# Five pairs of column groups a layer by seven block products instead of three, in both feed-forward layers of a one-core kernel

## What is computed

```python
def squared_relu_mlp(h, w1, w2):          # h 256 x 2048, w1 2048 x 8192, w2 8192 x 2048
    z = jax.nn.relu(h @ w1)
    return (z * z) @ w2
...
        x = x + squared_relu_mlp(rms_norm(x, ffn_norm[i]), w_ff1[i], w_ff2[i])
```

## Time and profile before

| | us |
|---|---|
| median of 3 runs (2959.05 to 2961.48) | 2959.76 |
| the profiled execution's own time | 2960.76 |
| its span, first to last instruction | 2959.0 |
| TensorE busy | 2916.3 |
| VectorE busy | 2055.5 |
| ScalarE busy | 1616.3 |

### The profile page before, as it was taken

How to read it: one execution, slowest core, us unless ns; L and a number is a source line. 1 busy time by engine, 2 the same in 40 slices (tenths; PEclk the granted TensorE clock), 3 DMA queues, 4 the chain that set the end, 5 groups by cost and what they waited for, 6 DMA issues and landing times.

```text
span 2959.0 us, 35189 instructions
## 1 busy us (share of the span) xinstructions
PE 2916.3 (99%) x12996; PEld 2400.2 (81%) x12996; DVE 2055.5 (69%) x2679; ACT 1616.3 (55%) x2134; POOL 634.5 (21%) x1257
## 2 busy tenths in 40 slices
PE   8999999999999999999999999999999999999998
PEld 7888888888888778788788888888888887878887
DVE  6547777777866777876777777756557777887555
ACT  6435555555554566755555555545444446775433
POOL 0003312213043310013203122133324663100210
PEclk9999999999999999999999999999999999999999
DMA  7546777778777655556777778776876776666774
GB/s 263 165 151 203 237 248 250 246 244 255 243 223 243 205 170 164 164 174 203 228 256 253 251 242 253 246 219 211 239 216 200 219 227 190 207 206 206 249 254 157
DMA packets 358156, 649.53 MB, mean 220 GB/s; under 512 B 38624, under 2 KB 63584, under 8 KB 357216
## 3 DMA queue, kind: packets, MB, share of 16 engines
q1 hardware_dynamic: 312976, 578.89, 61.7%
q0 software_dynamic: 44432, 67.45, 7.2%
q10 hardware_dynamic: 576, 0.94, 0.1%
HBM read 598.89 MB, written 10.49 MB: 206 GB/s over the span
## 4 chain that ended last, share of the span: by engine, by line
PE 73%; DVE 14%; DMA 7%; ACT 4%; issue 2%; DVEq 0%; ACTq 0%
PE acc L2093 21%; PE acc L2095 21%; PE acc L2094 21%; DMA raw<-in_w_ff 6%; DVE wlo L1457 5%; ACT whi L1086 1%; DVE wlo L1450 1%; PE tp L2130 1%; PE tp L2132 1%; PE tp L2131 1%; DVE mkv L1472 1%; DVE ob L1900 1%; PE tp L2299 1%; PE sd L2193 0%; PE sd L2218 0%
## 5 line engine op out<-in xcount | busy, mean ns | idle before, releaser
L1457 DVE TENSOR_TENSOR wlo<-raw,whi 128x1024 fp32r<-128x1024 f32 x920 | 1110.7, 1220 | 548.4 <-ACT whi L1086 544.0
L2093 PE MATMUL acc<-whi,set_hi 128*128 128x512 f32 x3696 | 1459.4, 395 | 20.8 <-DVE wlo L1457 15.4
L2095 PE MATMUL acc<-whi,set_lo 128*128 128x512 f32 x3696 | 1440.3, 390 | 0.0
L2094 PE MATMUL acc<-wlo,set_hi 128*128 128x512 f32 x3696 | 1439.8, 390 | 0.0
L1086 ACT ACTIVATE whi<-raw 128x1024 fp32r<-128x1024 f32 x920 | 959.4, 1057 | 684.1 <-PE acc L2095 378.3
L2093 PEld LDWEIGHTS acc<-whi,set_hi 128*128 128x128 f32 x3696 | 694.8, 188 | 182.8 <-DVE wlo L1457 27.1
L2095 PEld LDWEIGHTS acc<-whi,set_lo 128*128 128x128 f32 x3696 | 694.5, 188 | 146.2
L2094 PEld LDWEIGHTS acc<-wlo,set_hi 128*128 128x128 f32 x3696 | 695.0, 188 | 143.3 <-issue 1.9
L1050 POOL DMA_DIRECT2D u<-u x832 | 406.8, 497 | 1447.5 <-DVE u L1648 1337.9
L1450 DVE SCALAR_TENSOR_TENSOR wlo<-raw,par,whi 128x512 fp32r<-128x512 f32 x160 | 111.7, 747 | 47.1 <-ACT whi L1089 46.3
L1089 ACT ACTIVATE whi<-raw,par 128x512 fp32r<-128x512 f32 x160 | 104.2, 715 | 22.4 <-PE acc L2095 10.9
(11 more groups left out here) (332 smaller groups left out, 2121.3 us busy)
## 6 DMA issues: line engine op xcount, KB each, us to landing
raw<-in_w_ff SPq DMA_DIRECT2D x560, 512.0 KB, 4.7
raw<-in_w_in SPq DMA_DIRECT2D x248, 512.0 KB, 4.5
raw<-in_w_out SPq DMA_DIRECT2D x96, 512.0 KB, 4.4
u<-u POOLq DMA_DIRECT2D x832, 32.0 KB, 4.2
raw<-in_w_mem_kv SPq DMA_DIRECT2D x32, 512.0 KB, 4.3
raw<-in_w_proj_a SPq DMA_DIRECT2D x32, 512.0 KB, 4.7
raw<-in_w_proj_b SPq DMA_DIRECT2D x32, 512.0 KB, 6.9
raw<-in_w_kv SPq DMA_DIRECT2D x48, 256.0 KB, 3.3
```

What stands on the lines that cost most here:

```text
L1457: V.tensor_tensor(wlo[:, c], src, whi[:, c].bitcast(f32), ALU.subtract).then_inc(w_lo, 1)
L2093: T.matmul(o, h[:, tok], whi[:, c], start=first, stop=False)
L2094: T.matmul(o, h[:, tok], wlo[:, c], start=False, stop=False)
L2095: ins = T.matmul(o, l[:, tok], whi[:, c], start=False, stop=last)
```

## The change

`PAIRS = (0, 2, 1, 2)` gives the number of pairs in each chunk of a layer, before it was in effect (0, 1, 1, 1). Chunks 1 and 3 are now made by two pairs each and have no whole slab of the first product; chunk 2 stays at one. Pairs of one layer follow each other without a gap, so odd pairs use the PSUM quarters in another order (`bank`), a pair's p1 waits on `part_n2` of the one before and its p5 on `part_n1`, and `part_p1` waits for `part_relu`. The turn of z stands one slab later behind the square, with 7 slabs from turn to split. The diff, cut to what matters:

```diff
 FF2_PAIR = ((0, 1, 2, 3, 4, 5), (6, 7))
+FF2_LATE = ((0, 1, 2, 3), (4, 5), (6, 7))
+FF2_EVEN = ((0, 1), (2, 3), (4, 5), (6, 7))
+
+
+PAIRS = (0, 2, 1, 2)
 
 
 STAGES = ("p1", "p2", "p5", "p3", "p6", "p7", "p4")
...
+    def seven(layer, chunk, src, col, first, last):
+
+        p = sc.pair_of(layer, chunk, src, col, first, last)
+        pair = sc.pairs[p]
+        sc.at("act", pair.end("p1") + 5, "part_p1", p)
+        sc.at("dve", pair.end("p2") + 3, "part_c11", p)
+        sc.at("act", pair.end("p5") + 3, "part_p5", p)
+        sc.at("dve", pair.end("p6") + 3, "part_q", p)
+        return p
+
+    def drain(p, of, rst, z, kt, turn, split):
+
+        pair = sc.pairs[p]
+        add = pair.end("p7") + 3
+        if of == "n1":
+            add = max(pair.end("p4") + 3, add + 5)
+        sc.at("dve", add, "part_" + of, p)
+        sc.at("act", add + 2, "relu_" + of, p, rst)
+        sc.at("act", add + 2, "part_square", p, of, sc.staged, sc.tails)
+        sc.turned(max(turn, add + 3), split, ("staged", sc.staged), z, kt)
+        sc.staged += 1
+        if of == "n2":
+            sc.at("act", add + 3, "part_p7", p, sc.staged)
+
     def ffn(layer, rst, a, z, next_rst, next_gain):
 
-        for c in range(NCHUNK):
-            halved = c > 0
-            gs = [sc.group(f"w_ff1{layer}", 0, D * c + GW * i, a) for i in range(2 if halved else 0, 4)]
+        waiting = []
+        for c, count in enumerate(PAIRS):
+            gs = [sc.group(f"w_ff1{layer}", 0, D * c + GW * i, a) for i in range(2 * count, 4)]
             if c == 0:
                 sc.fed_late(gs[0])
                 v = S * gs[0]
@@ -386,39 +415,36 @@
                 for n in range(4):
                     sc.at("act", v + (13, 14, 16, 17)[n], "sum_hi", layer, n)
                     sc.at("dve", v + (14, 15, 17, 18)[n], "sum_lo", layer, n)
-            else:
+            elif count == 1:
                 v = S * gs[0]
-                pair = sc.pairs[p]
-                for of, kt, add, square, turn, split in (
-                        ("n2", 0, pair.end("p7") + 3, pair.end("p7") + 6, pair.end("p7") + 6, v + 1),
-                        ("n1", 4, pair.end("p4") + 3, pair.end("p4") + 6, v + 2, v + 9)):
-                    sc.at("dve", add, "part_" + of, p)
-                    sc.at("act", add + 1, "relu_" + of, p, rst)
-                    sc.at("act", square, "part_square", p, of, sc.staged, sc.tails)
-                    sc.turned(turn, split, ("staged", sc.staged), z, kt)
-                    sc.staged += 1
-                    if of == "n2":
-                        sc.at("act", square + 1, "part_p7", p, sc.staged)
+                p, = waiting
+                drain(p, "n2", rst, z, 0, f + 11, v + 1)
+                drain(p, "n1", rst, z, 4, v + 2, v + 9)
             for i, g in enumerate(gs):
-                turn, split = S * (g + 1) + 1, S * (g + 2) + 1
-                if halved:
-                    turn, split = S * (g + 1) + 2, S * (g + 2) + 2
-                sc.at("act", S * (g + 1) + 1, "epi_relu2", g, rst, sc.staged, sc.tails)
-                sc.at("act", turn, "epi_square", g, sc.tails)
-                sc.turned(turn, split, ("staged", sc.staged), z, 4 * i + (8 if halved else 0))
+                e = S * (g + 1)
+                late = 1 if count else 0
+                sc.at("act", e + 1, "epi_relu2", g, rst, sc.staged, sc.tails)
+                sc.at("act", e + 1 + late, "epi_square", g, sc.tails)
+                sc.turned(e + 2 + late, e + 9 + late, ("staged", sc.staged), z, 4 * (2 * count + i))
                 sc.staged += 1
             fs = [sc.group(f"w_ff2{layer}", D * c, GW * i, z) for i in range(4)]
-            sc.weave(fs[0], fs[1], FF2_PAIR)
-            if c < NCHUNK - 1:
-                v = S * fs[0]
-                p = sc.pair_of(layer, c + 1, a, v - (14 if halved else 12), v + 26)
-                pair = sc.pairs[p]
-                sc.at("act", pair.end("p1") + 3, "part_p1", p)
-                sc.at("dve", pair.end("p2") + 3, "part_c11", p)
-                sc.at("act", pair.end("p5") + 3, "part_p5", p)
-                sc.at("dve", pair.end("p6") + 3, "part_q", p)
-            for n, left in ((0, 2), (4, 1), (12, 0)):
+            f = S * fs[0]
+            sc.weave(fs[0], fs[1], FF2_PAIR if count < 2 else FF2_LATE)
+            at_need = ((0, 2), (4, 1), (12, 0)) if count < 2 else ((0, 3), (2, 2), (8, 1), (12, 0))
+            for n, left in at_need:
                 sc.groups[fs[n // S]].need[n % S] = [("tail_lo", sc.tails - left)]
+            more = PAIRS[c + 1] if c < NCHUNK - 1 else 0
+            if more == 1:
+                waiting = [seven(layer, c + 1, a, 0, f - (11, 14, 2)[count if c else 0], f + 26)]
+            elif more == 2:
+                sc.weave(fs[2], fs[3], FF2_EVEN)
+                first, middle = (f - 21, f + 6) if c else (f - 11, f + 9)
+                p = seven(layer, c + 1, a, 0, first, middle - 1)
+                q = seven(layer, c + 1, a, 2 * GW, middle, f + 29)
+                drain(p, "n2", rst, z, 0, f + 11, f + 23)
+                drain(p, "n1", rst, z, 4, f + 24, f + 29)
+                drain(q, "n2", rst, z, 8, f + 31, f + 37)
+                drain(q, "n1", rst, z, 12, f + 38, f + 44)
             for i, g in enumerate(fs):
                 e = sc.end(g)
                 sc.epilogue(g, "add", GW * i)
...
-        bank_a, bank_b, bank_c, bank_d = tp[:, 0:GW], tp[:, GW:2 * GW], sd[:, 0:GW], sd[:, GW:2 * GW]
+        quarters = tp[:, 0:GW], tp[:, GW:2 * GW], sd[:, 0:GW], sd[:, GW:2 * GW]
+
+        def bank(p, stage):
+
+            n = {"p1": 0, "p6": 0, "p4": 0, "p2": 1, "p7": 1, "p5": 2, "p3": 3}[stage]
+            return quarters[(2, 3, 1, 0)[n] if p % 2 else n]
...
                 act.wait_ge(mm, sc.pairs[p].last("p1"))
-                A_(first_c[:], bank_a, ACT.Copy).then_inc(sm["part_p1"], 1)
+                if p:
+                    act.wait_ge(sm["part_relu"], 2 * p)
+                A_(first_c[:], bank(p, "p1"), ACT.Copy).then_inc(sm["part_p1"], 1)
...
                 if part.j == 0:
                     if stage == "p1" and p:
+                        pe.wait_ge(sm["part_n2"], p)
+                    elif stage == "p5" and p:
                         pe.wait_ge(sm["part_n1"], p)
```

More of the change, by code:

```diff
@@ L101, with __init__ @@
 class Pair:
-    def __init__(self, layer, chunk, src, first):
-        self.layer, self.chunk, self.src, self.first = layer, chunk, src, first
+    def __init__(self, layer, chunk, src, col, first):
+        self.layer, self.chunk, self.src, self.col, self.first = layer, chunk, src, col, first
         self.parts = {}
@@ L132, in __init__, with pair_of @@
         self.stream = []
-    def pair_of(self, layer, chunk, src, first, last):
+    def pair_of(self, layer, chunk, src, col, first, last):
         p = len(self.pairs)
-        pair = Pair(layer, chunk, src, not any(q.layer == layer for q in self.pairs))
+        pair = Pair(layer, chunk, src, col, not any(q.layer == layer for q in self.pairs))
         self.pairs.append(pair)
@@ L830, in block_of @@
             pair = sc.pairs[part.pair]
-            row, col = P * (k * NK // 2 + SLAB_K * part.j), D * pair.chunk + GW * (1 - n)
+            row, col = P * (k * NK // 2 + SLAB_K * part.j), D * pair.chunk + pair.col + GW * (1 - n)
             return W[f"w_ff1{pair.layer}"][row:row + SLAB_K * P, col:col + GW].rearrange("(t p) n -> p t n", p=P)
@@ L1103, in part_p1 @@
                 act.wait_ge(mm, sc.pairs[p].last("p1"))
-                A_(first_c[:], bank_a, ACT.Copy).then_inc(sm["part_p1"], 1)
+                if p:
+                    act.wait_ge(sm["part_relu"], 2 * p)
+                A_(first_c[:], bank(p, "p1"), ACT.Copy).then_inc(sm["part_p1"], 1)
             def part_p5(p):
                 act.wait_ge(mm, sc.pairs[p].last("p5"))
-                A_(mixed_c[:], bank_c, ACT.Copy).then_inc(sm["part_p5"], 1)
+                A_(mixed_c[:], bank(p, "p5"), ACT.Copy).then_inc(sm["part_p5"], 1)
             def part_p7(p, staged):
@@ L1114, in part_p7 @@
                 act.wait_ge(sm["staged"], staged)
-                A_(stage_a[:, GW:2 * GW], bank_b, ACT.Copy).then_inc(sm["part_p7"], 1)
+                A_(stage_a[:, GW:2 * GW], bank(p, "p7"), ACT.Copy).then_inc(sm["part_p7"], 1)
             def relu_n2(p, k):
@@ L1512, in part_c11 @@
                 dve.wait_ge(sm["part_p1"], p + 1)
-                V.tensor_tensor(first_c[:], bank_b, first_c[:], ALU.add).then_inc(sm["part_c11"], 1)
+                V.tensor_tensor(first_c[:], bank(p, "p2"), first_c[:], ALU.add).then_inc(sm["part_c11"], 1)
             def part_q(p):
@@ L1518, in part_q @@
                 dve.wait_ge(sm["part_p5"], p + 1)
-                V.tensor_tensor(mixed_c[:], bank_a, mixed_c[:], ALU.add).then_inc(sm["part_q"], 1)
+                V.tensor_tensor(mixed_c[:], bank(p, "p6"), mixed_c[:], ALU.add).then_inc(sm["part_q"], 1)
             def part_n2(p):
@@ L1524, in part_n2 @@
```

(15 more changed lines are left out.)

## The result

The changed kernel takes 3017.3 us (median, 3015.8 to 3020.5) against 2959.6 on the same chip: a ratio of 1.0196, interval 1.018 to 1.0212. It is **58 us slower**, where 2950 us was forecast and 2982 was the upper end of the range. 21.8 us of TensorE's work did go away, so some 80 us were lost elsewhere.

A forecast was written before the change was run, and what follows sets the result against it. TensorE, busy 99% of the span, was taken as the bound. 2960.76 - 21.8 (matmuls saved) + 9 (stalls) + 2 (turns) + 1 (clock) = 2951.0 us profiled, 1.0 above the median, so 2950; range 2939 to 2982.

The forecast's parts named there:

- A: Slabs 112 to 119, 19 slots: TensorE 1.93 us a slot, VectorE's work 1.95, w 0.15; late by 3.2 us.
- B: Slabs 120 to 141, 51 slots: TensorE 1.95 us a slot, VectorE's work 1.74, w 0.30; late by 4.6 us.
- M: Slabs 144 to 167, the middle pair: TensorE 2.04 us a slot, VectorE's work 1.70, w 0.30; not late.
- C: Slabs 171 to 221: TensorE 2.01 us a slot, VectorE's work 1.70, w 0.30; not late.
- The turns: z of the last chunk part, split at the very slab needing it: 1 us at one place a layer, 2 in all.
- the waits between pairs: Waits between neighbouring pairs, on steps passed one slab earlier: 0, at worst 1 us each in six places.
- The clock: One TensorE gap long enough to bring half the clock, priced at 1 us in the sum.
- w: VectorE's idle time a slot, added to its work: bounds 0 and 0.49 us, taken as 0.15 or 0.30.
- the first 11 slabs: Start of the first pair: TensorE 1.91 us a slot against VectorE's work of 1.46, said to have room.
- The lead of 3.3 us: VectorE's splits ahead of TensorE by up to 3.7 us; 3.3 taken to absorb the first lateness of A and B.
- the slower one: Rival that feeding becomes the bound: w 0.40 everywhere gives 2980 us, the bound of 0.49 gives 3020; chance 0.27.
- landings stretch: The slower rival's reason for w of 0.40 everywhere: loads take longer to land than the 4.7 us before.

The follow-up runs named there:

- half_part_loads: The changed kernel with the loads of all parts but p1 halved to 256 KB, every instruction kept: 2946.5 us, ratio 0.9955 to the kernel before.

## Why the prediction was wrong

**What held.** Comparing stretch by stretch was the right place to look. So were 96 matmuls at 0.2266 us and VectorE's work a slot (A 1.94 against 1.95, B 1.75 against 1.74, M 1.74 and C 1.73 against 1.70). The turns and the waits between pairs cost nothing that shows, where I had put 2 us for the turns. The clock fell once more, as the sum had it for 1 us.

**The step that failed is w**, VectorE's idle time a slot, and what I did with it. I took it as a piece that is added to VectorE's work: 0.15 in A, 0.30 in B, M and C, and none that mattered in the first 11 slabs. It was 0.21, 0.35, 0.43, 0.38 and 0.63. It is no piece of its own: it is what is left of a turn of the ring when VectorE's work is taken out. Where VectorE has less to do it grows, and the pace stays at 2.10 to 2.17. So "the first 11 slabs have room" and "M and C are not late" were both false: they were late by 2.9, 5.4 and 12.3 us, as much as A and B together (15.6) and 5 more. The lead of 3.3 us that should have swallowed the first of it was gone before A began: TensorE already waits 1.10 us for a split at 374.19 us.

The number was in hand. I worked out 2.15 us a slot for the first pair of before and read it as TensorE's pace. The feeding side had none to spare: VectorE's lead fell from 3.71 us to 0.05 there. Between those two splits lie 19 slots in the trace, so they came every 2.36 us while TensorE used one every 2.17, and ScalarE waited for TensorE for only 1.1 us of those 44.8. The w of 0.30 came from 21 slots in 43 us instead, 2.05 a slot, in a window that has splits 1.14 us apart at both ends. With 1.85 to 2.05 wanted of a feeder that gives about 2.15, no stretch could keep up. A check over the whole layer would have shown it: the layer after the change has 316 slots, and 316 x 2.15 = 679 us, against about 680 us of TensorE's time in a layer before. By the feeding pace alone there was nothing to gain.

**The rival that came true** is the slower one, w from 0.40 to 0.49 for 2980 to 3020 us, at a chance of 0.27. Its mechanism was named rightly in part: a chain through loads and splits. Its cause was not: "landings stretch". The median landing of a feed-forward load is 4.7 us in both kernels. Nor was its sum right where w was: w is 0.40 on average over the five stretches (539.0 us less 438.4 of VectorE's work, over 254 slots), for which the rival gives 2980 us. It took three leads of 3 us a layer off, 18 us in all, which were not there, and left the first 11 slabs out. The Trainium skill ("DMA: Bandwidth & Descriptors", Latency and other measured facts) puts HBM's latency at 0.2 us on average and 2 us at high load. I let it speak for longer landings after the change, and my 0.6 us a slot for it has no working. No such growth showed in the median from before to after. Landings do grow with the loads under way, from 3.8 to 5.5 us as shown under half_part_loads, but they did so in both kernels. Of its other signs one came: idle time over 40 us before the first matmul line, and it was 60.5. VectorE's waits on loads over 0.4 us a slot did not: they were 0.21 in A (4.2 us) and 0.15 in B (8.0 us). In A they are all of w; in B the waits for copies, 9.9 us, are more.

**Split of the cost**, by the experiments: of the 76 us between the changed kernel and the one without chain operations, 18 us for VectorE's work and 58 us for loads and copies that wait through the chain operations. By place, of the 58 us by which the whole is slower: 40 us for the two pairs of chunk 1 and 18 for those of chunk 3. Of a landing of 4.8 us, 3.8 is what a load takes with no other weight load under way, and 1.0 comes with the others. The most direct test of the loop, a ring of more than four places, was not run.

## What to carry to other kernels

For a ring of n places, add up one place's turn (issue, landing, each serial step until it is free) and divide by n: with these step times that is the fastest pace a slot can have, however idle the engines are. It holds where each step follows the one before at once, which the trace must show. Compare it with what the consumer wants before work is taken from the consumer. A feeder whose lead shrinks to nothing while the consumer runs at full speed has no pace to spare; free a place after its last reader before asking more of it.

## What the runs showed of the hardware that I had not expected

**A short stall costs more than its row.** TensorE's idle time (span less busy) grew from 42.7 us to 85.7, by 43, yet the profiled execution lost 77. The stalls, intervals between matmul starts with idle time in them, went from 37 to 129. Timeline of TensorE in the changed kernel:

```profile
415.00 0.39 PE L2166 MATMUL tp<-whi,sum_lo 128*128 128x512 f32 x1
417.36 0.47 PE L2126 MATMUL acc<-whi,set_hi 128*128 128x512 f32 x1 [1.97 <-DVE wlo L1490]
417.67 0.39 PE L2127 MATMUL acc<-wlo,set_hi 128*128 128x512 f32 x1
417.90 0.40 PE L2128 MATMUL acc<-whi,set_lo 128*128 128x512 f32 x1
...
418.60 0.63 PE L2128 MATMUL acc<-whi,set_lo 128*128 128x512 f32 x1
419.02 0.63 PE L2126 MATMUL acc<-whi,set_hi 128*128 128x512 f32 x1
```

The matmul of 415.00 would have been followed at 415.23, so 2.13 us were lost and 1.97 are shown, since the idle time is counted from a modelled end 0.39 us after the start. The first matmul after the stall then takes 0.31 us to the next, not 0.23. That is 0.24 us beside the row. Over all starts of both traces, the 92 more stalls make 15 us by the first of these and 9.5 by the second, and the clock makes 1.6; some 7 us are left, spread over other intervals a little longer than 0.2266.

**The clock after such a gap.** From 418.60 the starts are 0.43 us apart, not 0.23: the lower of the clock's two levels, 1.2 GHz instead of 2.4. The window behind the gap, with the granted clock after POOL's column:

```profile
418.00:422.00 4.00, 4.00 (x12) 3.09 (x11) 3.27 (x4) 1.55 (x2) 0.00 (x0) 0.57 0.80 265
```

12 matmuls in 4 us, where the full clock gives 17.7: 1.3 us. Of the two gaps of before with nearly this length, one was followed by half the clock and one wasn't; the length of the last gap does not tell which.
